# One 2048-column VectorE subtraction for the low part of each weight unit, with one signal, in a fused two-block transformer kernel

## What is computed

```
h = adaln(rms_norm(x, g_mix), sh1, sc1)
proj = h @ w_in
...
x = x + gt1[:, None, :] * (mixed @ w_out)
h = adaln(rms_norm(x, g_mlp), sh2, sc2)
u = jnp.square(jax.nn.relu(h @ w_up))
x = x + gt2[:, None, :] * (u @ w_down)
```

## Time and profile before

| | before |
|---|---|
| median of 3 runs | 1591.01 us (1589.99 to 1592.7) |
| the profiled execution: its time | 1592.92 us |
| the profiled execution: its span, first to last instruction | 1591.1 us |
| mean granted TensorE clock | 0.976 |
| busy: TensorE, VectorE, ScalarE, GpSimd | 95%, 80%, 55%, 15% of the span |

### The profile page before, as it was taken

One profiled execution on the slowest core, in us unless ns is written; L12 is line 12 of the kernel. 1 busy time (PEld: TensorE's weight loads), 2 busy tenths in 40 slices (PEclk: granted clock), 3 DMA queues, 4 the chain that ended last, 5 costly groups with the idle time before them and its releaser, 6 DMA issues.

```text
span 1591.1 us, 24600 instructions
## 1 busy us (share of the span) xinstructions
PE 1512.4 (95%) x10058; PEld 1301.4 (82%) x10058; DVE 1273.9 (80%) x1861; ACT 882.1 (55%) x1220; POOL 245.7 (15%) x191
## 2 busy tenths in 40 slices
PE   6899989999999998899999899999999988899998
PEld 2889888999989987799998668888877856678887
DVE  1858898888887875699996669999968877579995
ACT  3537536445443653355443657778754465458774
POOL 3250000000005000000001410025631310310041
PEclk9999999999999999899999999999998989999999
DMA  9854497999955537678876179999983812689993
GB/s 332 287 180 131 145 327 267 328 318 328 329 190 159 160 127 244 212 268 288 291 265 212 42 269 373 401 370 372 375 303 117 317 43 95 223 313 375 366 373 145
DMA packets 184704, 408.11 MB, mean 256 GB/s; under 512 B 7608, under 2 KB 136048, under 8 KB 166032
## 3 DMA queue, kind: packets, MB, share of 16 engines
q1 hardware_dynamic: 170688, 334.53, 59.7%
q0 software_dynamic: 11264, 63.49, 10.7%
q10 hardware_dynamic: 2640, 8.52, 1.4%
HBM read 397.08 MB, written 9.45 MB: 255 GB/s over the span
## 4 chain that ended last, share of the span: by engine, by line
PE 77%; DVE 13%; ACT 5%; DMA 2%; issue 2%; POOL 1%; SPq 0%; ACTq 0%; POOLq 0%; DVEq 0%
PE psum L736 73%; DVE acc L2057 3%; DVE w_lo L2034 3%; DVE gu_lo L2068 1%; PE psum L1451 1%; ACT w_hi L1528 1%; DMA raw<-in_w_ada 1%; DVE tmp L2086 1%; ACT att_room L1958 1%; DVE x L2169 1%; DVE h_lo L2095 1%; PE psum L1272 1%; PE psum L1237 1%; DVE tmp L2272 1%; POOL tmp L2645 1%
## 5 line engine op out<-in xcount | busy, mean ns | idle before, releaser
L2034 DVE TENSOR_TENSOR w_lo<-raw,w_hi 128x1024 fp32r<-128x1024 f32 x250 | 307.1, 1270 | 67.7 <-ACT w_hi L1528 67.5
L736 PE MATMUL psum<-h_hi,w_lo 128*128 128x256 f32 (+1 forms) x1280 | 339.5, 288 | 1.0 <-DVE w_lo L2034 1.0
L736 PE MATMUL psum<-h_lo,w_hi 128*128 128x256 f32 (+1 forms) x1280 | 339.9, 289 | 0.0
L1528 ACT ACTIVATE w_hi<-raw 128x2048 fp32r<-128x2048 f32 x125 | 238.7, 1912 | 102.5 <-DMA raw<-in_w_up 47.1
L736 PE MATMUL psum<-h_hi,w_hi 128*128 128x256 f32 (+1 forms) x1280 | 263.1, 298 | 8.2 <-DVE tmp L2272 5.7
L736 PEld LDWEIGHTS psum<-h_hi,w_lo 128*128 128x128 f32 x1280 | 249.2, 195 | 2.5 <-DVE w_lo L2034 1.2
L736 PEld LDWEIGHTS psum<-h_lo,w_hi 128*128 128x128 f32 x1280 | 249.2, 195 | 1.5
L2057 DVE SCALAR_TENSOR_TENSOR acc<-raw,cond,acc 128x1024 f32<-128x1024 f32 x182 | 239.9, 1326 | 4.5
L736 PEld LDWEIGHTS psum<-h_hi,w_hi 128*128 128x128 f32 x1280 | 198.4, 195 | 32.1 <-issue 18.5
L2068 DVE TENSOR_TENSOR gu_lo<-raw,gu_hi 128x2048 fp32r<-128x2048 f32 x92 | 206.6, 2287 | 14.7 <-ACT gu_hi L1545 14.7
L1545 ACT ACTIVATE gu_hi<-raw 128x2048 fp32r<-128x2048 f32 x96 | 178.3, 1907 | 5.0 <-DMA raw<-in_moe_wg 5.0
(11 more groups left out here) (287 smaller groups left out, 2740.9 us busy)
## 6 DMA issues: line engine op xcount, KB each, us to landing
raw<-in_w_ada SPq DMA_DIRECT2D x48, 1024.0 KB, 6.9
raw<-in_w_mod SPq DMA_DIRECT2D x48, 1024.0 KB, 5.6
raw<-in_w_in SPq DMA_DIRECT2D x34, 1024.0 KB, 5.7
raw<-in_w_up SPq DMA_DIRECT2D x32, 1024.0 KB, 6.0
raw<-in_w_down SPq DMA_DIRECT2D x32, 1024.0 KB, 6.3
raw<-in_moe_wg SPq DMA_DIRECT2D x32, 1024.0 KB, 7.4
raw<-in_moe_wu SPq DMA_DIRECT2D x32, 1024.0 KB, 7.8
dn_raw<-in_moe_wd SPq DMA_DIRECT2D x32, 1024.0 KB, 7.2
```

The source lines that it names most:

```text
L736: return e.matmul(o, lhs, rhs, start=start, stop=stop, skip_group_check=True)
L1528: e.activation(flat_unit(w_hi[:, split_slot(u)]), raw[:, slot, :], ACT.Copy).then_inc(*w_rounded.on(u))
L2034: e.tensor_tensor(flat_unit(w_lo[:, split_slot(u), k]), raw[:, slot, part], plain(flat_unit(w_hi[:, split_slot(u), k])), ALU.subtract).the ...
```

## The change

The subtraction becomes one instruction of 2048 columns with one signal, `w_rest` of (u, 1). The first value, of half 0, is gone, and the three places in TensorE's program that asked for half k // 4 (or part) now ask for (g, 1), the whole unit. The pieces for experts (`split_expert`, `gu_lo`) were whole already and stay as they are.

```diff
@@ TensorE's program, product
-                            e.wait_ge(*w_rest.at(g, k // 4))
+                            e.wait_ge(*w_rest.at(g, 1))
@@ TensorE's program, attention outputs
-                                e.wait_ge(*w_rest.at(g, part))
+                                e.wait_ge(*w_rest.at(g, 1))
@@ VectorE's program, feed
                         e.wait_ge(*w_rounded.at(u))
-                        for half in range(2):
-                            k = slice(half * DT // 2, (half + 1) * DT // 2)
-                            part = slice(half * UNIT // 2, (half + 1) * UNIT // 2)
-                            e.tensor_tensor(flat_unit(w_lo[:, split_slot(u), k]), raw[:, slot, part],
-                                            plain(flat_unit(w_hi[:, split_slot(u), k])), ALU.subtract).then_inc(
-                                *w_rest.on(u, half))
+                        e.tensor_tensor(flat_unit(w_lo[:, split_slot(u)]), raw[:, slot, :],
+                                        plain(flat_unit(w_hi[:, split_slot(u)])), ALU.subtract).then_inc(*w_rest.on(u, 1))
```

## The result

| | before | after |
|---|---|---|
| median of 7 runs each, same chip | 1591.01 us (1589.99 to 1595.14) | 1587.02 us (1585.16 to 1588.90) |
| ratio after to before | | 0.9968, 95% interval [0.9953, 0.9983] |
| the profiled execution: span | 1591.1 us | 1583.4 us |
| mean granted TensorE clock in it | 0.976 | 0.980 |

The page of the changed kernel: span and busy time, then the chain that ended last by engine and by line.

A forecast was written before the change was run, and what follows sets the result against it. The prediction took the kernel as bound by TensorE, with stretches bound by VectorE. Only the chain's 20 x 0.070 = 1.4 us counted, all else nothing: 1591.01 - 1.4 = 1589.6 us, range 1587.3 to 1592.8 us.

The forecast's parts named there:

- the price of a unit: VectorE's subtraction: one 2048-column instruction instead of an overlapping pair saves 0.070 us per unit (2.355 to 2.285 us).
- 20 x 0.070 = 1.4 us: Chain that ended last: some 20 units' worth of subtraction lie on it, so the span shortens by 1.4 us.
- The first rival (off the path): ScalarE's rounding or a transfer ends the waits instead, so the saving is off the path: 1591.0 us; chance 0.20.
- So 1.07 us cost nothing: Unit 1: TensorE's first load of w_lo comes 1.07 us later, covered by its 2.52 us standstill from 61.35 us.
- the sum: Whole kernel: only the chain's 1.4 us counted, so the median goes from 1591.01 to 1589.6 us.
- the rival on the clock: After 63.87 us: shorter idle time may avoid TensorE's half clock, 1.7 us more gain, 1586.2 to 1587.9 us; chance 0.06.
- Where this touches TensorE is unit 124: GpSimd's sum of squares at 1352.71 us waits for the whole subtraction, at most 1.57 us later for TensorE.
- I take nothing: GpSimd's longer wait at unit 124: at most 0.34 us left, counted as zero, with 0.3 us kept in the range.
- VectorE's busy time: All 125 units: one instruction for two takes 8.75 us off VectorE's busy time, most of it not on the path.
- the low end at 1587.3: Range's faster end: the start-price rival's 1587.6 us, less 0.3 us for the spread of runs.
- Start price: Rival: each removed instruction start saves its full 0.153 us, 22 times on the chain, 3.4 us, 1587.6 us; chance 0.07.
- MLP: Rival: TensorE waits for the whole signal in each layer's MLP, 4.2 us slower, 1595.2 us; chance 0.07.

The follow-up runs named there:

- e5: Kernel before, but each subtraction is four instructions of 512 columns, signals still after each half: 1.0037 of before, mean +6.6 us.
- e3: Changed kernel, but unit 1 keeps two instructions and two signals: 1.0003 of before, mean +0.2 us.
- e10: Changed kernel, but unit 1 has two instructions and two signals, units 115, 116, 123, 124 two instructions and one signal: 0.9993 of before, mean -1.1 us.
- e6: Kernel before, but one instruction with one signal in the 21 units on its chain, unit 1 not among them: 1.0008 of before, mean +0.4 us.
- e1: Changed kernel run again, nothing altered, beside the kernel before: 0.9989 of before, mean -2.5 us.
- e9: Changed kernel run a third time, nothing altered, beside the kernel before: 0.9966 of before, mean -5.4 us.
- e4: Changed kernel, but units 115, 116, 123 and 124 keep two instructions, with one signal: 0.9972 of before, mean -4.6 us.
- e8: Same kernel as e4, run again in another batch: 0.9968 of before, mean -4.2 us.
- e12: Same as e6, but unit 1 also in one instruction with one signal: 0.9983 of before, mean -3.4 us.
- e2: Kernel before, still two instructions in each unit, but TensorE waits for the whole unit's signal: 0.9993 of before, mean -1.0 us.
- e11: Changed kernel, but units 115 and 116 keep two instructions, with one signal: 0.9979 of before, mean -4.0 us.
- e7: Kernel before, plus four matmuls with unused results in TensorE's idle time ahead of the norm factors' product: 0.9999 of before, mean -1.1 us.

## Why the prediction was wrong, point by point

**Right: the price of a unit.** "The gain of one unit is therefore 2.355 - 2.285 = 0.070 us": 2.286 us measured, the step 2.20 us, and e5 shows the same 0.07 us for each further seam.

**The chain: there, not settled in size.** "20 x 0.070 = 1.4 us." e3, e10 and e6 have this term without the late unit 1. At equal clock they are 0.6, 1.0 and 1.0 us faster (± 0.6 each), together 0.8 ± 0.3; in plain run times +0.2, -1.1 and +0.4 us. The changed kernel's 1.5 ± 0.4 us at equal clock is no measure of it, since it also holds the moved stretch and GpSimd's longer wait. The first rival (off the path) isn't needed, though the plain times of these three alone wouldn't refute it.

**Failed: "So 1.07 us cost nothing."** This is the step that was wrong: the sum puts nothing for what TensorE's clock does behind the later load. The load was covered, as I wrote, but covering it was not all that it did: the longer wait (TensorE's weight loads stood still for 2.25 us, before for 1.18) moved the half-clock stretch from behind the norm factors to before them, under the same cover. I had that as the rival on the clock with the right price (1.7 us; 1.5 in the traces) and gave it 0.06. Its picture was off too: I had the idle time shrink to 1.45 us and the fall perhaps not come; the fall came earlier and the idle time went to nothing. That unit 1 decides is shown by three pairs of kernels that differ in it alone: after (e1, e9) against e3, e4 and e8 against e10, e12 against e6. They differ by 4.1 ± 1.2, 3.3 ± 1.1 and 3.7 ± 1.4 us, and by 1.0 ± 0.7, 1.4 ± 0.7 and 1.4 ± 0.8 us at equal clock. The second figures are the moved stretch; the rest is that the kernels with the late unit 1 lose less clock. In the profiles the first two pairs show 3.0 us, 143.7 against 146.8 us, and the third 1.5 us.

**Failed, with less effect: GpSimd.** "Where this touches TensorE is unit 124" missed the norm ahead of unit 115, where TensorE's wait grew from 1.82 to 3.42 us; I had looked for loads of `w_lo` that come close, in all 125 units, but for GpSimd's operations beside a subtraction only at one. The Trainium skill, "SBUF — State Buffer", section "SBUF: two separate sides", has an exclusive lock for the whole instruction; the trace agrees: the first square ends more than 1.1 us after the subtraction, and the two take 4.09 us, 1.27 us each undisturbed. At unit 124 the wait was 3.05 us for 2.09, within the bound. "I take nothing" was wrong for the segment (2.3 to 2.8 us). For the whole the price is not clear of the error: 0.4 ± 1.0 us, 0.8 ± 0.5 at equal clock.

**Mis-sized: VectorE's busy time**, 18.3 us for 8.75. The other half is contention that ended: a whole instruction isn't interrupted by GpSimd, a pair was. (One that GpSimd is ahead of still waits: up to 3.39 us in after.)

**The range.** I took the spread of before from three runs, 2.7 us, and let 0.3 us of it into the low end. 35 runs span 10.0 us with a standard deviation of 2.7. With that spread the median of a few runs alone wanders by about 1 us, and the low end at 1587.3 should, as an estimate, have stood near 1586 even with the sum as it was. That the time fell 0.3 us below the range and not into it was decided by this spread: e1's 0.9989 of 1591.01 us would be 1589.3 us, almost the forecast, and e9's 0.9966 is 1585.6. What doesn't hang on it is the mechanism: the mean of 4.2 us is three times the sum.

**Rivals.** Start price: refuted by the step and by e5. MLP: no second unit waited; unit 86's load came at 688.29, its subtraction ended at 688.06. Clock: its price came true (1.5 us in the traces, 1.0 to 1.4 us in the runs at equal clock), and the kernels with it lost less clock besides.

**What stays open.** The late unit 1 alone gives 1.0 us (e2), the instruction alone nothing (e3), both 4.2 us. At equal clock they add up: 1.0 and 0.6 us against 1.5. The excess is lost clock: 39.0 us in before, 38.8 in e2, 40.0 in e3, 38.5 in e10, 41.5 in e6, but 33.6 to 37.4 us, in the mean 35.9, where the late unit 1 and 22 or more whole instructions come together (e1, e9, e4, e8, e11, e12). Why both together lose some 4 us less clock than either alone isn't shown. The half-clock stretches that the profiles show beyond the first 17 units differ between executions of one kernel, so they would have to be counted over many profiles; one for each kernel doesn't tell.

## What to carry to other kernels

Before costing a later load at nothing, look at what TensorE's clock does behind the next wait: idle time that is covered may also take a half-clock stretch with it, to a place where it is free or to one where it is not. When one VectorE instruction replaces two, list every GpSimd operation that can run beside it and who waits for it; and try the halves there. Here they took TensorE's wait back from 3.42 to 1.82 us, but the runs show no gain clear of the error. A saving of one us is not a forecast when executions of one kernel differ by ten: take the spread from many runs, and compare both the plain times and those at equal granted clock: the second show what a moved stretch is worth, the first also what the kernel gains or loses in clock. And a segment of a trace has to start ahead of the half-clock stretch that is to be priced, or it hides it (e6).

## What the runs showed of the hardware that was not expected

- In the first 17 units, idle time of TensorE of 2.0 to 2.7 us went with 3.4 or 6.8 us at 1.2 GHz (granted clock 0.50) that began between 0.5 us before its end and 2.4 us after it: at unit 1's wait 3.4 us in all eight profiles with the late load, at the norm factors' wait 3.4 us in before and e6 and 6.8 us in e3, e10 and e5. In before, after and e6 it began behind the idle time and TensorE was busy throughout. With the idle time at that place cut to 0.79 us (e7) there was none.
- A lost us of clock lengthened a run by 0.67 ± 0.03 us (243 runs), not by one.
- Where VectorE's subtraction and GpSimd meet, who began first keeps its full speed: VectorE 2.28 us and GpSimd 4.09 for two squares in after, GpSimd's first square 1.27 and VectorE 3.94 for its pair in e4.
